# Identity products on TensorE in the waits at stage seams and in the router's tail

## The reference

```python
def first_block(x, ...):
    ...
        proj = xn @ w_in[l]
        ...
        mixed = jnp.concatenate([ret, rw], axis=-1).astype(x.dtype)
        h = h + mixed @ w_out[l]
        h = h + hier_moe(rms_norm(h, norm2_gain[l]), ...)
    return rms_norm(h, final_norm_gain)
```

## Time and profile before

| What | Value |
|---|---|
| Runs | 2706.67 us median of 3 (2704.95 to 2709.91) |
| Profiled execution | 2709.03 us, its span 2707.3 us |
| Mean granted TensorE clock over the span | 0.972 |
| TensorE, products | busy 2517.7 us (93%), 14812 instructions |
| VectorE | busy 1964.9 us (73%), 2667 instructions |
| ScalarE | busy 1411.4 us (52%), 2182 instructions |
| GpSimd | busy 601.5 us (22%), 554 instructions |

### The profile page before, as it was taken

One profiled execution on the slowest core, in us unless ns is written; L12 is line 12 of the kernel. 1 busy time (PEld: TensorE's weight loads), 2 busy tenths in 40 slices (PEclk: granted clock), 3 DMA queues, 4 the chain that ended last, 5 costly groups with the idle time before them and its releaser, 6 DMA issues. The chain is left out here.

```text
span 2707.3 us, 39686 instructions
## 1 busy us (share of the span) xinstructions
PE 2517.7 (93%) x14812; PEld 2066.7 (76%) x14813; DVE 1964.9 (73%) x2667; ACT 1411.4 (52%) x2182; POOL 601.5 (22%) x554
## 2 busy tenths in 40 slices
PE   8999978888897799999996899889999999999998
PEld 7988856666676688888885888668887788888776
DVE  5532157888845799999996834778778988888586
ACT  5111157888612687877875432357744433344444
POOL 0000035666601110000001500220001334432231
PEclk9999989999998899999998999999999999999999
DMA  5555321211263799999996321000221232325866
GB/s 187 192 201 221 122 90 36 74 45 62 85 233 140 270 407 414 412 414 419 412 418 235 138 58 46 1 33 32 57 94 55 78 93 62 93 85 172 210 131 183
DMA packets 168279, 454.06 MB, mean 168 GB/s; under 512 B 15260, under 2 KB 95568, under 8 KB 154832
## 3 DMA queue, kind: packets, MB, share of 16 engines
q1 hardware_dynamic: 146048, 384.62, 38.7%
q0 software_dynamic: 16336, 46.67, 6.2%
q10 hardware_dynamic: 5760, 20.97, 1.9%
HBM read 373.05 MB, written 79.17 MB: 167 GB/s over the span
## 5 line engine op out<-in xcount | busy, mean ns | idle before, releaser
L135 PE MATMUL psum<-part,expert_x_high 128*128 128x512 f32 x520 | 206.8, 398 | 2.9 <-issue 1.5
L137 PE MATMUL psum<-part,expert_x_low 128*128 128x512 f32 x520 | 203.8, 392 | 0.0
L135 PE MATMUL psum<-project_w_high,high 128*128 128x448 f32 (+1 forms) x512 | 194.6, 380 | 3.5 <-DVE low L399 3.5
L136 PE MATMUL psum<-project_w_low,high 128*128 128x448 f32 (+1 forms) x512 | 193.7, 378 | 0.0
L137 PE MATMUL psum<-project_w_high,low 128*128 128x448 f32 (+1 forms) x512 | 193.5, 378 | 0.0
L130 DVE TENSOR_TENSOR expert_down_low<-expert_down,expert_down_high 128x2048 fp32r<-128x2048 f32 x62 | 139.3, 2288 | 39.0 <-ACT expert_down_high L125 39.0
L130 DVE TENSOR_TENSOR expert_gate_low<-expert_gate,part 128x2048 fp32r<-128x2048 f32 x64 | 143.8, 2288 | 7.1 <-ACT part L125 7.0
L130 DVE TENSOR_TENSOR expert_up_low<-expert_up,part 128x2048 fp32r<-128x2048 f32 x64 | 143.8, 2289 | 1.0 <-ACT part L125 1.0
L135 PE MATMUL psum<-part,ffn_w_high 128*128 128x512 f32 x352 | 138.2, 392 | 5.8 <-DVE ffn_u L4715 4.1
L136 PE MATMUL psum<-ffn_b_low,ffn_w_high 128*128 128x512 f32 x352 | 137.5, 391 | 0.0
L135 PE MATMUL psum<-down_right_high,down_left_high 128*128 128x512 f32 x308 | 121.5, 395 | 9.8 <-DVE down_right_low L130 6.2
(11 more groups left out here) (780 smaller groups left out, 7471.4 us busy)
## 6 DMA issues: line engine op xcount, KB each, us to landing
expert_gate<-in_w_gate_dram SPq DMA_DIRECT2D x32, 2048.0 KB, 10.0
expert_up<-in_w_up_dram SPq DMA_DIRECT2D x32, 2048.0 KB, 9.9
expert_down<-in_w_down_dram SPq DMA_DIRECT2D x32, 2048.0 KB, 10.6
ffn_w<-in_ffn_w_up_dram SPq DMA_DIRECT2D x44, 512.0 KB, 4.6
y_rows<-expert_y ACTq DMA_DIRECT2D x32, 512.0 KB, 10.7
down_right_raw<-in_ffn_w_down_dram SPq DMA_DIRECT2D x44, 256.0 KB, 3.6
hidden_rows<-ffn_hidden SPq DMA_DIRECT2D x20, 512.0 KB, 2.8
ffn_hidden<-hidden_rows SPq DMA_DIRECT2D x20, 512.0 KB, 6.7
```

What stands on the lines that cost most here:

```text
L135: pe.matmul(out, left[0], right[0], start=start, stop=False)
L136: pe.matmul(out, left[0], right[1], start=False, stop=False)
L137: return pe.matmul(out, left[1], right[0], start=False, stop=stop)
```

## The change

A new helper issues products of the identity with itself, 128 by 128 with 128 columns, into a PSUM bank that no one reads before it is next written. It is called at fifteen places of TensorE's lists. In the router one wait is added ahead of the first call there. Nothing else differs.

```diff
+def keep_busy(pe, bank, ident, count):
+
+    for _ in range(count):
+        pe.matmul(bank[:, 0:P], ident[:], ident[:], start=True, stop=True)
...
+            keep_busy(pe, bank[0], ident, 24)
             pe.wait_ge(const, 16 * len(cn.loads))
             turn_lo(0, 0)
+            keep_busy(pe, bank[0], ident, 4)
             for n in range(3):
                 lift(n, 0, 0)
+            keep_busy(pe, bank[0], ident, 8)
             pe.wait_ge(w_added, 1)
             run_ends(0, 0)
             run_sums(0, 0)
             run_sum_before(0, 0)
+            keep_busy(pe, bank[0], ident, 8)
...
             turn_heads(5, lambda n: head(ry_raw, n, P), 4, last_turned)
+            keep_busy(pe, bank[3], ident, 10)
             pe.wait_ge(rw_last, 1)
             turn_heads(6, lambda n: head(y_raw, n, P), 4, last_turned)
+            keep_busy(pe, bank[3], ident, 12)
...
             turn(TT - 1)
+            pe.wait_ge(added, TT)
+            keep_busy(pe, bank[1], ident, 4)
             score(TT - 1)
+            keep_busy(pe, bank[1], ident, 26)
             rank(1)
+            keep_busy(pe, bank[1], ident, 48)
             pe.wait_ge(in_place_ready, 2)
...
             last.then_inc(ids_made, 1)
+            keep_busy(pe, bank[1], ident, 54)
...
             turn_x(pe, 0, 0, 0)
+            keep_busy(pe, bank[2], ident, 6)
             each_step(pe, step)
...
+            keep_busy(pe, bank[0], ident, 100)
             turn(0)
+            keep_busy(pe, bank[0], ident, 10)
...
             queries(TT - 1)
+            keep_busy(pe, bank[0], ident, 4)
             keys(TT - 1)
+            keep_busy(pe, bank[0], ident, 8)
```

## The result

The changed kernel takes 2718.8 us (median of 14 runs, 2714.4 to 2728.0), the kernel before 2709.4 (14 runs, 2702.5 to 2715.3) on the same chip: a ratio of 1.0041 with a 95% interval of 1.0031 to 1.0052, so 8.4 to 14.1 us slower. The forecast was 2714, range 2702 to 2722, with slower the likeliest. Direction and range held; the loss is some 4 us larger than the sum of +6.9. The profiled execution, 2714.42 us with a span of 2712.7, is the fastest of the 14.

A forecast was written before the change was run, and what follows sets the result against it. TensorE, busy 93% of the span, was taken to bound the kernel, with half-speed clock at some stage seams. Terms 2.4-0.4-0.5+6.4-1.0 = +6.9 us gave 2715.9 for the profiled execution and a median forecast of 2714 us, range 2702 to 2722.

The forecast's parts named there:

- mix start: Opening of the mix stage: 24, 4, 8 and 8 products delay the first transposes; +2.4 us, bounds +1.0 and +3.5.
- mix end: End of the mix: the 12 close the stage 1.5 us later, the router opens at full speed; -0.4 us.
- router's tail, expert: Router's tail into first expert: faster work against fillers that outlast waits; -0.5 us, taken between -2.6 and +3.1.
- projection start: Projection's opening: the 100 end at 1496.3, 7.3 us late, and VectorE's loop keeps its delay whole; +6.4 us.
- attention start: Attention's opening: scores at full speed spare VectorE's wait, the barrier is 0.5 us later; -1.0 us.
- Price of a product: Each added identity product: two records, 0.223 us at full speed and 0.447 at half speed.
- The first rival: All added products: each costs one record, 0.109 us, so the kernel is faster, 2695 us; chance 0.14.
- Do they lift the clock?: Added products at the stage openings: the clock returns after 5.0 us of them, range 4.1 to 6.2.
- the third rival: All added products: identity products don't lift the clock, so the kernel is far slower, 2782 us; chance 0.05.
- half speed until the 26 are running: Router's tail: the clock stays low until the filler ahead of the rank; +3.1 us for tail and first expert.
- The 54's 3.0 us of barrier: Router's last filler, 12.1 us long, was to make the stage's barrier 3.1 us late, eating the expert's 3.2.
- the 24's lateness: Mix start: the 24 end at 364.9, 5.7 us after the transposes could start; VectorE's sigmoid input comes 3.7 us late.

The follow-up runs named there:

- g3: The kernel before with only the 10 and 12 products at the mix's end; ratio 0.9984 (0.9970 to 0.9997).
- e1: The changed kernel without its 100 and 10 products at the projection's start; ratio to the kernel before 1.0018 (1.0005 to 1.0032).
- f3: The changed kernel without the 24, 4, 8 and 8 products at the mix's start; ratio to the kernel before 1.0021 (1.0011 to 1.0031).
- f4: The changed kernel as it is, timed again with a second profiled execution; ratio to the kernel before 1.0049 (1.0033 to 1.0066).
- e3: The kernel before with only the router's tail products (4, 26, 48, 54) and the 6 ahead of the first expert; ratio 1.0015 (1.0001 to 1.0029).
- e4: The changed kernel with all counts fitted to the waits its trace shows, 10 more in the tail; ratio to the kernel before 1.0003 (0.9987 to 1.0019).
- f2: The kernel before with the fitted tail (10, 4, 24, 34, 30), 6 for the first expert, attention's 4 and 8; ratio 0.9995 (0.9985 to 1.0005).
- g1: The kernel before with fitted router's tail, first expert's 6, attention's 4 and 8, and 10 and 6 at mix end; ratio 0.9977 (0.9964 to 0.9991).
- f1: The kernel before with only the 24, 4, 8 and 8 products at the mix's start; ratio 1.0018 (1.0005 to 1.0031).
- g4: The kernel before with the mix start's 24, 4, 8, 8 and 6 more in a first-turn wait; ratio 1.0013 (1.0001 to 1.0025).
- e2: The kernel before with only the 100 and 10 products at the projection's start; ratio 1.0026 (1.0011 to 1.0041).
- g2: Fitted tail, first expert, attention and mix-end products, with ScalarE's second gate split moved behind its places; ratio to the kernel before 0.9974 (0.9960 to 0.9987).

## Why the prediction was right, and where it was wrong

Its terms, against what the stages give with and without the products (us):

```
                        forecast   measured   from
mix start                 +2.4       +3.2     mix: 389.1 against 385.9, the means above
mix end                   -0.4       -1.6     g3: seam +1.6, router -3.2
router's tail, expert     -0.5       +2.8     router: changed, e1, f3, f4, mean 144.6, against g3's 139.4;
                                              expert and projection: e1, e3, e4, f2, g1, 810.7,
                                              against before, f1, g3, g4, 813.1
projection start          +6.4       +6.5     e2: 819.6 against 813.1
attention start           -1.0       -1.4     attention 141.0 against 142.6, mixers 100.0 against 99.8
sum                       +6.9       +9.5     timed: 8.4 to 14.1
```

The second mixers' means leave out g2's 103.6, and each stage is a mean of few executions or a single one, so a term is good to about 1 us.

**Price of a product.** Right: two records each, and at full speed 10.72 us from the first of the 48 to the id product behind them (866.45 to 877.17), 0.223 each, as taken. The first rival, one record, is out.

**Do they lift the clock?** Yes, and the third rival is out: in the projection the clock is up 5.8 us after the first of them (1471.1 to 1476.9), in the mix 4.1 us (356.6 to 360.7). The forecast had 4.1 to 6.2. The Trainium skill, "TensorE: Matmul & The Clock Gate", Part 4 (PE-mode transpose), says that the full clock doesn't engage for TensorE's transpose mode, which doesn't count as busy in the same way. In the kernel before the clock went from 0.50 to 1.00 behind sixteen transposes, at 376.1; that is one place, and these runs add nothing to it, since they changed products and no transpose.

**Projection start.** Right in mechanism and size: the 100 end at 1496.3, as forecast to a tenth, and VectorE's loop keeps the lateness whole.

**Attention start.** Right in mechanism: VectorE's second scores come 2.8 us after the opening instead of 4.2 and wait for nothing, where the earlier trace rows had 1.47 us. The 4 and 8 cost 0.2 us in the second mixers where 0.5 was charged.

```profile
1812.38 0.29 DVE L3970 TENSOR_TENSOR psum<-psum,attention_future 128x128 f32<-128x128 f32 x1
```

**Router's tail.** The case was priced and not chosen. The prediction gave +3.1 for "half speed until the 26 are running", -2.6 for full speed, and took -0.5 between. In three of the four executions with the change's tail and mix end the clock fell at the wait of 2.87 us ahead of the last turn and stayed down until the 26 (changed, e1, f3: 145.3 to 146.7 us); in f4 it fell for 3.4 us only (141.0). The row for that wait was there, and the sentence that nothing is added ahead of it too. Between two cases of which each is likely, the middle is the one value that didn't come. The 54's 3.0 us of barrier came as forecast; the first expert gave back 2.4 us of the 3.2. In e3, with full speed from within the score on, the stages give +0.7 where the prediction had -1.3 for that case.

**Mix start.** Here the step failed, not by its size but by its mechanism. The prediction let the clock come up after 5 us and stay; the 24's lateness was all that it charged. The lateness came (VectorE's mix_p_t at 367.22, 3.0 us later after the opening than before, where 3.7 was forecast), but in the profiled execution it was made up: the first turn, from the first to the second scaled key, took 34.4 us instead of 37.1. In f1 it took 35.5, and in f4 and e1 the clock fell again in that turn, which then took 39.3. That the measured mean, +3.2, is near the forecast is luck: at the second turn one execution of the five (f1) had lost about what was charged, two had lost nothing and two 6 us. The median's extra loss over the profiled execution is likely mostly this, on the word of two executions of the changed kernel.

**Mix end.** The seam's +1.6 is the forecast's 1.5. The gain behind it was too small in the forecast: in g3 the first addition comes 5.8 us after the opening instead of 7.7, 1.9 as forecast, and 1.3 us more come later; the kernel before had another stretch of 3.4 us at half speed there (from 761.8) that g3 hasn't.

**What the success rests on.** The projection's term alone, right in mechanism and size, makes the kernel slower. The errors of the other terms (+0.8, -1.2, +3.3, -0.4) partly cancel, and the range of 20 us would have held them all. The forecast of 2714 also started from a median of three runs, 2706.67, where fourteen gave 2709.4.

## What to carry to other kernels

A product that keeps a clock up stands in the same queue as the work it is for: count the products against the shortest wait seen, at the clock that they will have there, since one that outlasts its wait delays all that is queued behind it and the stage's barrier. Put it where the next work is bound by TensorE (here the router's opening, the first expert, attention); at the projection VectorE bounds, and products there gained nothing: 70 left the stage as it was, 100 cost 6.5 us. When a tail gets faster, look at what its other engines have queued ahead of the pieces it needs: here a split waiting for a store of 16 us.

## What the runs showed that was not expected

The same kernel has its slow stretches at different places in different executions: the changed kernel's first turn ran at 1.00 in one and at 0.50 for 17.1 us in another (mix 384.5 and 392.6 us). And the last stage, in which nothing was changed, varied by 10 us over fourteen executions (758.0 to 768.3). A single profiled execution gives stages and mechanisms; a sum over its stages isn't yet the median.

The mean granted clock of every timed run shows how the profiled one stands among them. Of the changed kernel's 14 runs the nine at 0.988 or more took 2714.4 to 2720.3 us, the five at 0.986 or less 2723.7 to 2728.0; the profiled one had 0.991. Within each of these kernels a run with a lower clock is on the whole a slower run. Between kernels that doesn't hold: the kernel before runs at about 0.972 and is faster than the changed one at 0.988, since the clock that the products buy isn't worth what they hold up.
